# The first expert group of each half of a routed-expert loop begins with three shared-lane steps, and the step of one expert alone comes behind it

## What is computed

```
scores = sigmoid(x @ router_w);  biased = scores + router_bias
# 4 of 8 groups by the sum of their two best, then the 8 best experts of these
gates  = one_hot(eidx) * (sel / sum(sel) * 2.5)
hb     = silu(x @ ex_w1[e]) * (x @ ex_w3[e])          # 1024 -> 256, for each expert e
routed = sum over e of (hb * gate) @ ex_w2[e]         # 256 -> 1024
```

## Time and the profile before

| | us |
|---|---|
| runs of the kernel before | 998.61, 995.68, 997.41 (median 997.41) |
| the profiled execution, its own time | 996.36 |
| its span in the profile | 994.6 |
| TensorE busy in the span | 937.3 (94%) |
| VectorE busy | 484.5 (49%) |
| GpSimd busy | 367.5 (37%) |
| mean granted TensorE clock | 0.983 |

### The profile page before, as it was taken

How to read it: one execution, slowest core, us unless ns; L and a number is a source line. 1 busy time by engine, 2 the same in 40 slices (tenths; PEclk the granted TensorE clock), 3 DMA queues, 4 the chain that set the end, 5 groups by cost and what they waited for, 6 DMA issues and landing times.

```text
span 994.6 us, 16457 instructions
## 1 busy us (share of the span) xinstructions
PE 937.3 (94%) x6042; PEld 426.2 (43%) x6042; DVE 484.5 (49%) x1312; ACT 152.5 (15%) x373; POOL 367.5 (37%) x452
## 2 busy tenths in 40 slices
PE   7999999999998999998999997989979999899896
PEld 5777878755453333232233332322322233333442
DVE  6756753546766443434334442333431434432885
ACT  3011134301112111111011110101100111113322
POOL 6203431301147345433444433444442455421231
PEclk9999999999999999999999998999989999999999
DMA  8303230720497999999999999999999999978922
GB/s 266 110 12 106 85 103 11 233 75 21 159 359 312 349 381 413 412 411 413 412 405 412 414 413 413 399 407 402 410 414 375 392 410 412 412 285 358 419 83 84
DMA packets 76132, 297.51 MB, mean 299 GB/s; under 512 B 15638, under 2 KB 26078, under 8 KB 49165
## 3 DMA queue, kind: packets, MB, share of 16 engines
q1 hardware_dynamic: 60149, 258.68, 66.5%
q0 software_dynamic: 15904, 37.79, 9.9%
HBM read 276.56 MB, written 31.50 MB: 310 GB/s over the span
## 4 chain that ended last, share of the span: by engine, by line
PE 64%; DMA 19%; DVE 7%; issue 4%; POOL 3%; DVEq 1%; SPq 1%; POOLq 0%; ACT 0%; ACTq 0%
PE bank L2728 23%; PE bank L2326 17%; PE bank L2723 8%; DMA arena<-in_ex_w 6%; PE bank L2823 6%; DMA ring<-in_ex_w 5%; DMA arena<-xs_dram,slot 5%; PE bank L2570 2%; DMA arena<-y_dram 2%; POOL arena L1071 1%; POOL arena L963 1%; DMA ring<-in_w_in 1%; PE bank L2775 1%; PE bank L2492 1%; PE bank L2332 1%
## 5 line engine op out<-in xcount | busy, mean ns | idle before, releaser
L2728 PE MATMUL bank<-arena 128*32 128x512 f32 x1440 | 270.1, 608 | 10.3 <-issue 5.5
L1071 POOL DMA_INDIRECT arena<-xs_dram,slot x192 | 206.3, 1074 | 68.1 <-issue 57.6
L2728 PE MATMUL bank<-ring,arena 128*32 128x512 f32 x864 | 213.3, 606 | 3.6 <-DMA arena<-in_ex_w 3.6
L1087 POOL DMA_INDIRECT y_dram<-arena,outrow x46 | 47.1, 1024 | 271.5 <-DVE slot L2086 223.1
L2728 PE MATMUL bank<-xT,arena 128*32 128x512 f32 x576 | 115.7, 609 | 6.7 <-DMA ring<-in_ex_w 6.7
L2728 PEld LDWEIGHTS bank<-arena 128*32 128x32 f32 x1440 | 67.5, 112 | 112.1 <-issue 104.9
L2100 DVE STREAM_TRANSPOSE arena<-arena 128x1024 f32<-128x1024 f32 x48 | 59.7, 1244 | 86.9 <-DMA arena<-xs_dram,slot 86.9
L2728 PE MATMUL bank<-mixpj,arena 128*32 128x512 f32 x384 | 84.7, 594 | 0.0
L2180 DVE COPY outrow<-yrow 128x1 int32<-128x1 int32 x46 | 7.1, 154 | 145.7 <-PE bank L2728 117.2
L2199 DVE SCALAR_TENSOR_TENSOR arena<-bank,gate,arena 128x256 f32<-128x256 f32 x46 | 22.3, 484 | 112.3 <-ACT arena L1333 112.1
L2728 PEld LDWEIGHTS bank<-ring,arena 128*32 128x32 f32 x864 | 50.9, 111 | 47.9 <-issue 43.3
(11 more groups left out here) (466 smaller groups left out, 1409.6 us busy)
## 6 DMA issues: line engine op xcount, KB each, us to landing
arena<-in_ex_w SPq DMA_DIRECT2D x78, 1024.0 KB, 22.2
ring<-in_ex_w SPq DMA_DIRECT2D x50, 1024.0 KB, 23.0
xT<-in_ex_w SPq DMA_DIRECT2D x28, 1024.0 KB, 19.3
mixpj<-in_ex_w SPq DMA_DIRECT2D x24, 1024.0 KB
arena<-y_dram SPq DMA_DIRECT2D x18, 1024.0 KB, 11.0
wide<-in_ex_w SPq DMA_DIRECT2D x12, 1024.0 KB, 25.4
ring<-in_w_in SPq DMA_DIRECT2D x4, 2048.0 KB, 9.0
ring<-in_w_out SPq DMA_DIRECT2D x2, 2048.0 KB, 10.6
```

The costliest lines, as they stand in the source:

```text
L1071: pool.indirect_dma_start(xg[b][:, 256 * a:256 * a + 256], None, xs_quarter, bass.IndirectOffsetOnAxis(slot[k][:, a:a + 1], 0), bounds_che ...
L1087: pool.indirect_dma_start(y_dram, bass.IndirectOffsetOnAxis(outrow[b][:, 0:1], 0), og[b], None, bounds_check=K * T - 1, oob_is_err=False). ...
L2728: ins = pe.matmul(b[t, :], lhs[:, t], rhs(home(own if lane < 3 else common)), start=start, stop=stop)
```

## The change

The string of a half becomes `PSPPQPPPSQQ`. Step 0 (23) now uses places 0 and 1, step 1 places 2 and 1, step 2 places 3 and 1, and step 3 (26) place 4 alone. From step 4 on each step uses the same places as before. `HOMES` is written anew to match: the order of homes in which the first five loads are issued stays 0, 1, 2, 4, 3, now for places 0 to 4 in order. The lists of refills that come out of it differ in two ways. Place 8 (40) is released after step 2 (25) and no longer after step 3 (26). And place 33, needed from step 24 before, is needed from step 23, while it is still released after step 21.

Since step 0 is now of kind P, its common expert's one-hot must be made ahead of the first pick, and step 1 shares it; the first pick has five matmuls more, and the pick of step 3, made in step 0, five fewer. `hits`, which shared its memory with the common one-hot's operands, moves to the memory of `hT`. A table constant for a second pass of the loop moves with the S kind.

```
-    HALF = expert_steps("SPPPQPPPSQQ")
+    HALF = expert_steps("PSPPQPPPSQQ")
...
-    HOMES = [0, 1, 2, 3, 4, 0, 1, 3, 2, 4, 0, 3, 1, 2, 4, 3, 0, 1, 2, 4, 3, 1, 0, 2, 4, 1, 3, 0, 2, 1, 3, 4]
+    HOMES = [0, 1, 2, 4, 3, 0, 2, 4, 1, 3, 0, 4, 1, 2, 3, 4, 0, 1, 2, 3, 4, 1, 0, 2, 3, 1, 4, 0, 2, 1, 4, 3]
...
-        hits_raw = ex(NE)
-        hits = hits_raw[0:NE, :]
+        hits = hT_raw[0:NE, 0:NE]
+        common_raw = ex(NE)
...
-            for p in (1, 2, 4, 3):
+            for p in range(1, FIXED):
                 if home(p) == 3:
                     after(sp, "sh", NP_ - 1)
...
             dve.wait_ge(s_split, 2)
-            one_hots(0, 0, 0, heads[0], None)
             dve.wait_ge(s_const, 5)
+            one_hots(0, 0, 0, heads[0], heads[1])
...
-            one_hots(0, 0, 1, heads[1], heads[2])
+            one_hots(0, 0, 1, heads[2], None)
...
-                                  (-4.0, -3.0, -3.0, -3.0, -3.0, -3.0)[k], None, ALU.add)
+                                  (-3.0, -3.0, -3.0, -3.0, -4.0, -3.0)[k], None, ALU.add)
...
-                pick(j + 1, j % 2, b, j, j > 0).then_inc(filled, 1)
+                pick(j + 1, j % 2, b, j, True).then_inc(filled, 1)
...
-                    pick(base + (j + 4), (j + 3) % 2, bank[7], j + 3, joins(j + 3) or j == 0).then_inc(s_psel, 1)
+                    pick(base + (j + 4), (j + 3) % 2, bank[7], j + 3, joins(j + 3)).then_inc(s_psel, 1)
```

More of the change, by code:

```diff
@@ L386, in decoder_step @@
         hu = ex(FF)
-        hT = ex(2 * P).rearrange("p (c t) -> p c t", t=P)
+        hT_raw = ex(2 * P)
+        hT = hT_raw.rearrange("p (c t) -> p c t", t=P)
         cols = [ex(NC) for _ in range(2)]
@@ L396, in decoder_step @@
         rank_row, keys = (ex(NE)[0:NE, :] for _ in range(2))
-        hits_raw = ex(NE)
-        hits = hits_raw[0:NE, :]
-        inqx = hits_raw[:, 0:NT * 3].rearrange("p (i a) -> p i a", a=3)
-        valqx = hits_raw[:, NT * 3:NT * 3 + NT * 3 * 6 // 2].bitcast(BF16).rearrange("p (i a c) -> p i a c", a=3, c=6)
+        hits = hT_raw[0:NE, 0:NE]
+        common_raw = ex(NE)
+        inqx = common_raw[:, 0:NT * 3].rearrange("p (i a) -> p i a", a=3)
+        valqx = common_raw[:, NT * 3:NT * 3 + NT * 3 * 6 // 2].bitcast(BF16).rearrange("p (i a c) -> p i a c", a=3, c=6)
         np_k, np_c = keys[0:1, :].bitcast(I32), rank_row[0:1, :]
```

## The result

The changed kernel took 1000.21 us (median of 10 runs, 997.40 to 1003.16), the kernel before 997.29 in 10 runs of the same session (994.91 to 999.18): a ratio of 1.0030, with a 95% interval from 1.0017 to 1.0042. So it is 2.9 us slower, just at the 0.3% that the prediction counts as no change, but its interval lies wholly above 1. The forecast was 997.5 with a range of 993.5 to 1002.0: the time lies in the range, 2.7 us above the forecast.

The account below looks back on a forecast made before the run. The prediction took the DMA stream of weights to bound the loop. A 2.0 us loss ahead of it less a 1.9 us gain from place 8's earlier load, with net 0 at step 23, gave +0.1 us: 997.5, range 993.5 to 1002.

Parts of the forecast that it names:

- Part 1: Work ahead of the loop: the extra common one-hot delays the first pick and all loads that wait for the loop.
- d: Loss ahead of the loop from the later own one-hot: 2.0 us, with ends 0.9 and 3.4.
- Part 2: First half: place 8 loaded one step earlier fills free DMA time from 346 to 358 us, a gain.
- f: Gain from place 8's earlier load: 1.9 us, low end 0.5, at most 5.1.
- the 400 that was named: Sign in the new profile: a rate near 400 GB/s in the 12 us behind place 8's load.
- Part 3: Beginning of the second half: a new 9.4 us wait at step 23 replaces two old waits and a slow mm1, net 0.
- the mark that the prediction had set for being wrong: Sign in the new profile: step 34 starts more than 3 us away from 743.
- The sum: Whole kernel: the stream and all behind it end d − f = +0.1 us later, giving 997.5 us.
- the prediction's own picture: Expert loop: it ends when the weight stream ends, and a moment with DMA idle is lost for good.
- The larger collision: Rival, ahead of the loop: second one-hot pays the full 3.28 us against GpSimd again; +2.9, 1000.4 us; chance 0.16.
- More filling: Rival, DMA stream: place 8's whole load fills holes, 5.1 us; −3.1, 994.3 us; chance 0.25.
- step 23's wait: Rival, second half: the new wait isn't swallowed; +7, 1004.5 us, or 1001 if half swallowed; chance 0.14.

Follow-up runs that it names:

- e4: The changed kernel with the shared expert's second group and its transposes ahead of the first pick, gate transposes between pick and order; 1.0002 of the kernel before, 997.89 us.
- e10: The kernel before with only TensorE's work ahead of the loop placed as in e4; 0.9983 of the kernel before, 996.96 us.
- e1: The kernel before, its own order of steps, homes and loads, with only the common one-hot made ahead of the first pick; 1.0027 of the kernel before, 1000.92 us.
- e3: The changed kernel with five idle matmuls on TensorE ahead of the first pick; 1.0013 of the kernel before, 999.93 us.
- e6: The changed kernel with two idle matmuls on TensorE ahead of the first pick; 1.0000 of the kernel before, 998.09 us.
- e12: e1 with two idle matmuls on TensorE ahead of the first pick; 1.0018 of the kernel before, 1000.02 us.
- e7: e4 with place 8 loaded one step later again, as before, and place 40 still early; 1.0009 of the kernel before, 998.71 us.
- e8: e4 with place 40 loaded one step later again, as before, and place 8 still early; 0.9994 of the kernel before, 998.03 us.
- e5: The kernel before with seven idle matmuls (6.18 us) on TensorE ahead of the first pick; 1.0050 of the kernel before, 1002.82 us.
- e9: e1 with TensorE's work ahead of the loop placed as in e4; 1.0003 of the kernel before, 998.19 us.
- e2: The changed kernel with places 8 and 40 loaded one step later again, as before; 1.0032 of the kernel before, 1000.72 us.
- e11: e4 with DVE's order of the experts made ahead of the index of step 0; 1.0011 of the kernel before, 998.99 us.

## Why the prediction was nearly right, by its steps

**Part 1, the mechanism right, the term d mis-sized.** "2.2 us later" for the own one-hot: measured 2.26, at the pick. "So d = 2.2 + 0.1 − 0.4 = 1.9, I say 2.0 us" is the step that fell short. It lets the delay of the pick go on unchanged, as if TensorE merely stood for 2.2 us. The wait of 2.35 us was followed by a clock of 0.50, which made the transposes and the shared expert's matmuls 2.3 us longer by mm1 of step 0, and the slow mm1 added 1.66. The waits of 1.2 to 1.3 us there, for the pick in e4 and for the order in before and e10, were not followed by it. In the time of the whole kernel d is 2.7 us (e1, 1.1 to 4.2), of which about 2.0 go back when the wait holds matmuls (e3, e6, e12). The prediction's own view of step 24 (mm1 in 10.02 us after a wait) had shown what a rest does to the clock, and was not applied to the new wait.

**Part 2, f = 1.9 too much.** The load did go one step earlier. Place 8's two loads follow those of place 7 in the queue of after:

```profile
351.79 0.81 SPq L727 DMA_DIRECT2D mixpj<-in_ex_w  x2
352.79 1.03 SPq L727 DMA_DIRECT2D arena<-in_ex_w  x2
```

But against before it is less early than "one step" says. Place 8's load is issued 56.30 us into the frame (352.79 − 296.49), and in before 60.09 (354.95 − 294.86): 3.8 us sooner, not the 11 of a step, since the late start took the rest. The rate in the 12 us behind its issue (351.8 to 363.8) is 360 GB/s, not the 400 that was named; that is reached in the 12 us that begin 1.8 us later. Still it did something: at 70 us into the frame after has moved 1.3 us more than e1, and e4 1.6 us more than e7, nearly the 1.9 of the forecast. The step that failed is that "the rest of place 8's load only lengthens the queue", as if that cost nothing. With it in front, the gather behind came about 3 us late, and the stream ran short some 10 us on. What is left at the end is 0.2 to 0.7 us, not to be told from 0; the low end of the prediction's range for f (0.5) was the better value.

**Part 3, right.** Step 23's wait came, 6.78 us of idle time (9.4 were forecast) before a slow mm1:

```profile
608.32 1.07 PE L2729 MATMUL bank<-ring,arena 128*32 128x512 f32 x3 [6.78 <-DMA arena<-in_ex_w]
...
631.66 1.92 PE L2729 MATMUL bank<-ring,arena 128*32 128x512 f32 x16 [2.00 <-DMA ring<-in_ex_w]
```

Against before in the frame, TensorE is 6.85 us late at step 22, 16.55 at step 23, and 6.68 at step 27: the new wait took the place of the two old ones, net 0. A third, of 2.00 us, at 631.66 for a w2 was not foreseen, and lies within that. Place 40 early costs and brings nothing (e8). At step 34 the wait has shrunk:

```profile
749.03 0.63 PE L2729 MATMUL bank<-mixpj,arena 128*32 128x512 f32 x3 [2.92 <-DMA ring<-in_ex_w]
```

It is 2.92 us instead of the 6.67 of the earlier trace rows, and starts 6.0 us later, 4.4 in the frame. This is the mark that the prediction had set for being wrong ("more than 3 us away from 743"), and by it the prediction's account is wrong, though its number is right. The cause is the late start of the loop rather than step 23: the silu of step 34 is 3.3 us late in the frame in after, and 4.0 in e1 and 5.8 in e5, which have no new wait at step 23.

**The sum, and where luck helped.** The forecast was d − f = 0.1 us, and 2.9 were measured. As far as such intervals tell, f has the larger share of the miss (0.2 to 0.7 for 1.9) and d the smaller (2.7 for 2.0). But step 0 began 4.59 us late at mm1 and was 6.25 late at its silu, two and three times the d of the forecast. By the prediction's own picture, in which such a loss is lost for good, the end should have been as late. Part of it was swallowed at the last steps, which the prediction doesn't have. In the frame after is 9.0 us behind before at the silu of step 43, and 5.0 at that of step 44. There before waited for weights, and ran mm1 at a clock that had fallen (0.83 from 860 to 870 us):

```profile
864.72 8.70 PE L2723 MATMUL bank<-arena 128*64 128x512 f32 x32 [2.99 <-DMA arena<-in_ex_w]
```

The changed kernel came later, didn't wait there, and ran it at the full clock:

```profile
872.95 7.09 PE L2724 MATMUL bank<-arena 128*64 128x512 f32 x32
```

So the time came near the forecast by luck: the start was worse than said, and the end more forgiving.

**The rivals.** The larger collision gave 1000.4, nearly the time that was measured, by a mechanism that isn't the one: the second one-hot took 2.29 us (302.57 to 304.86), not 3.28. More filling (994.3) did not occur, and step 23's wait was swallowed. The order of the steps itself, everything else equal, makes +0.3 (the change against e1), −0.1 (e4 against e9) and −1.8 us (e6 against e12) by the ratios, a mean of −0.5 that can't be told from 0.

**What stays open.** An mm1 of step 0 that begins 5.22 us late goes with 5.0 at the end in e5, one 4.18 to 4.59 late with 2.7 to 3.0 in e1 and the change: why these differ was not found. The intervals overlap (3.4 to 6.6 and 1.1 to 4.2 us in e5 and e1), so part of it may be scatter. It isn't the stream at the start: at 130 us into the frame it is 6.6 us behind before in e5 and 6.3 in e1. The reason of e10's gain was not found either, nor why TensorE's clock falls once more in mm1 of step 0 in some kernels (0.80 to 0.90 from 313 to 330 us in the change, e1, e2, e6, e7, e8, e10, e11, e12) and not in others (1.00 in before, e3, e4, e5, e9) though they wait alike, some 0.8 to 1.2 and 1.8 us, ahead of it; with one trace of each, it may as well change from one execution to the next.

## What to carry to other kernels

Price a new wait of TensorE as its length and then the clock behind it: look in the trace for the granted clock after the nearest waits of that length, and reckon the stage behind it at the low level. Such a wait can be filled, with the engine's own work from behind it or with matmuls that compute nothing; here this gave back 2.8 (e4) and 3.0 us (e6) of the change's 3.0. Where the clock hadn't fallen, in the kernel before, the same placing measured 1.7 us faster (e10), for a reason that isn't known. When a load is issued earlier into a shared stream, look at what is issued behind it: here a gather came late, and the 1.6 us gained were down to 0.3 some 60 us on.

## What the runs showed of the hardware

- 2 MB more of weights queued one step earlier went with a gather some 3 us later: the pick behind it waits 2.2 to 3.1 us in six kernels, against at most 0.35 in the eight where they were not.
